# The first microseconds of a streaming-encoder kernel: halves of x in another order, the first gain row by itself, a product entered operand by operand, and three products of zeros

## What is computed

```python
z = rmsnorm(h, ln_in) @ w_in          # (640 x 1024) @ (1024 x 2464)
c_q, c_kv, k_r, g_a, u_val, u_gate, g_c = jnp.split(z, [...], axis=-1)
... # latent attention from c_q, c_kv, k_r; a depthwise convolution of u_val * sigmoid(u_gate)
h = h + jnp.concatenate([y_a, y_c], axis=-1) @ w_out
h = h + sigmoid(rmsnorm(h, ln_pg) @ w_pg) * (p @ w_pe)
```

## Time and profile before

| | us |
|---|---|
| median of three runs | 815.36 |
| the profiled execution | 814.89 |
| span of its instructions | 813.1 |
| TensorE busy | 777.2 |
| VectorE busy | 568.1 |
| ScalarE busy | 412.4 |

### The profile page before, as it was taken

The page is one execution under the profiler, slowest core; times in us unless marked ns, Lnnn a source line. Parts: engine busy times, 40 slices in busy tenths (PEclk is TensorE's granted clock), DMA queues, the critical chain, the costliest instruction groups (busy, mean ns, idle before and its releaser), DMA issues.

```text
span 813.1 us, 10487 instructions
## 1 busy us (share of the span) xinstructions
PE 777.2 (96%) x3782; PEld 603.3 (74%) x3782; DVE 568.1 (70%) x1093; ACT 412.4 (51%) x944; POOL 54.6 (7%) x94
## 2 busy tenths in 40 slices
PE   6999999999999999999999999999999999999991
PEld 4799878666766578888888988775767666888881
DVE  3349988888885685546462999889788468655455
ACT  3565645654456562363375473556445547224534
POOL 5000123000000310000000012220000000000000
PEclk9999999999999999999999999999999999999996
DMA  9622222110000153322272232121000004341203
GB/s 303 199 74 78 73 68 82 36 52 27 26 1 1 54 192 130 120 76 78 77 247 69 78 95 73 47 70 52 28 27 0 1 27 142 105 138 57 78 1 129
DMA packets 40569, 65.26 MB, mean 80 GB/s; under 512 B 7774, under 2 KB 19898, under 8 KB 40502
## 3 DMA queue, kind: packets, MB, share of 16 engines
q1 hardware_dynamic: 37354, 58.45, 22.4%
q0 software_dynamic: 3104, 6.12, 2.5%
q10 hardware_dynamic: 60, 0.02, 0.0%
HBM read 57.86 MB, written 7.17 MB: 80 GB/s over the span
## 4 chain that ended last, share of the span: by engine, by line
PE 83%; DVE 8%; ACT 6%; issue 1%; DMA 1%; SPq 0%; DVEq 0%; ACTq 0%
PE acc L600 19%; PE acc L602 19%; PE acc L601 18%; PE sharedT L534 4%; PE acc L718 4%; PE sharedO L804 4%; DVE VT L1383 3%; PE sharedS L790 3%; PE sharedT L779 3%; PE sharedS L534 2%; PE sharedO L534 2%; PE sharedT L773 1%; ACT JUNK L953 1%; PE sharedS L766 1%; ACT SB L1146 1%
## 5 line engine op out<-in xcount | busy, mean ns | idle before, releaser
L600 PE MATMUL acc<-WHI,XHI 128*128 128x512 f32 (+1 forms) x720 | 302.9, 421 | 0.6 <-DVE XLO L1328 0.6
L602 PE MATMUL acc<-WHI,XLO 128*128 128x512 f32 (+1 forms) x720 | 279.1, 388 | 0.0
L601 PE MATMUL acc<-WLO,XHI 128*128 128x512 f32 (+1 forms) x720 | 278.5, 387 | 0.0
L1383 DVE SCALAR_TENSOR_TENSOR VT<-UX,CWT,VT 128x640 f32<-128x640 f32 x240 | 211.9, 883 | 5.1
L600 PEld LDWEIGHTS acc<-WHI,XHI 128*128 128x128 f32 x720 | 135.7, 189 | 39.1 <-issue 15.2
L1318 DVE SCALAR_TENSOR_TENSOR WLO<-WR,GT,WHI 128x512 fp32r<-128x512 f32 (+1 forms) x144 | 100.1, 737 | 86.0 <-ACT WHI L957 85.7
L602 PEld LDWEIGHTS acc<-WHI,XLO 128*128 128x128 f32 x720 | 135.5, 188 | 26.7
L601 PEld LDWEIGHTS acc<-WLO,XHI 128*128 128x128 f32 x720 | 136.0, 189 | 25.7 <-issue 3.8
L957 ACT ACTIVATE WHI<-WR,GT 128x512 fp32r<-128x512 f32 (+1 forms) x144 | 94.9, 711 | 105.5 <-PE acc L602 100.6
L957 ACT ACTIVATE PT<-sharedT 128x384 f32<-128x384 f32 (+1 forms) x80 | 35.7, 447 | 43.0 <-PE sharedT L534 41.9
L1146 ACT ACTIVATE SB<-SB,NBIAS 128x384 f32<-128x384 f32 (+1 forms) x80 | 45.7, 571 | 18.6 <-DVE NBIAS L1439 18.1
(11 more groups left out here) (191 smaller groups left out, 821.2 us busy)
## 6 DMA issues: line engine op xcount, KB each, us to landing
WR<-in_w_in_dram SPq DMA_DIRECT2D x32, 256.0 KB, 3.0
WR<-in_w_in_dram SPq DMA_DIRECT2D x16, 512.0 KB, 3.5
WR<-in_w_out_dram SPq DMA_DIRECT2D x16, 512.0 KB, 3.6
WR<-in_w_pg_dram SPq DMA_DIRECT2D x16, 512.0 KB, 3.6
WR<-in_w_in_dram SPq DMA_DIRECT2D x8, 416.0 KB, 3.6
residual_spill<-H SPq DMA_DIRECT2D x5, 512.0 KB, 3.3
H<-residual_spill SPq DMA_DIRECT2D x10, 256.0 KB, 3.3
H<-in_x_prompt_dram SPq DMA_DIRECT2D x4, 512.0 KB, 7.9
```

Source lines behind the costliest of these rows:

```text
L600: mm(out, hi, w_hi, start=(first and k == 0), stop=False)
L601: mm(out, hi, w_lo, start=False, stop=False)
L602: last = mm(out, lo, w_hi, start=False, stop=(final and k == 1))
L1383: ins = stt(out=out, in0=src, scalar=w, in1=out, op0=ALU.mult, op1=ALU.add)
```

## The change

It alters only how layer 0 starts:

- `FIRST` is another list. The left halves (g = 0) of all five tiles come first, with the quanta of piece 0 between them; piece 1 follows with the right halves. The last flip, `("x", 4, 1)`, is now the last entry. SyncE loads half tiles of 256 KB in the order of `FIRST`, with the three pieces after the first, the third and the sixth of them.
- `ln_in` signals its own semaphore `gain_in`. Its eight rows are turned alone right behind the first flip (bank `gain_in`); all thirty rows are turned after the whole of `FIRST`, and VectorE copies the 22 others to `GT` after `low(2)`.
- The first quantum waits for each operand by itself (`first_hi`, `first_lo`, `w_first`) instead of for the whole split piece.
- GpSimd clears 384 columns of `TH` first; TensorE multiplies those zeros three times (128x256, into `acc[4]`, which is started afresh later) before it waits for the identity.
- The cache loads of layer 0 wait until the last half tile of x has landed.

```diff
-FIRST = [("x", 0, 0), ("x", 0, 1), ("x", 1, 0), (0, 0), ("x", 1, 1), ("x", 2, 0), (0, 1), ("x", 2, 1), (1, 0), ("x", 3, 0),
-         (0, 2), ("x", 3, 1), (1, 1), ("x", 4, 0), (0, 3), ("x", 4, 1), (1, 2), (0, 4), (1, 3), (1, 4)]
+FIRST = [("x", 0, 0), ("x", 1, 0), (0, 0), ("x", 2, 0), (0, 1), ("x", 3, 0), (0, 2), ("x", 4, 0), (0, 3), (0, 4),
+         (1, 0), ("x", 0, 1), (1, 1), ("x", 1, 1), (1, 2), ("x", 2, 1), (1, 3), ("x", 3, 1), (1, 4), ("x", 4, 1)]
+FIRST_X = [step[1:] for step in FIRST if step[0] == "x"]
...
-                eng.dma_start(ROWS[g:g + n, :], a[name][l].rearrange("(k p) -> k p", p=P)).then_inc(rows_in, 16)
+                eng.dma_start(ROWS[g:g + n, :], a[name][l].rearrange("(k p) -> k p", p=P)).then_inc(
+                    gain_in if name == "ln_in" else rows_in, 16)
...
-                for t in range(TILES):
-                    sp.dma_start(H[:, t, :], x_rows(t)).then_inc(x_in[t], 16)
-                    if t in (0, 1, 3):
-                        piece((0, 1, None, 2)[t])
+                for t, g in FIRST_X:
+                    cols = slice(512 * g, 512 * (g + 1))
+                    sp.dma_start(H[:, t, cols], x_rows(t)[:, cols]).then_inc(x_in[g][t], 16)
+                    if (t, g) in ((0, 0), (2, 0), (0, 1)):
+                        piece(((0, 0), (2, 0), (0, 1)).index((t, g)))
...
+                    begin = (i, t, k) == (0, 0, 0)
+                    if begin:
+                        pe.wait_ge(half_hi, 1)
+                        pe.wait_ge(first_hi, 1)
+                    elif (i, t, k) == (0, 0, 1):
+                        pe.wait_ge(split_ready, 1)
                     mm(out, hi, w_hi, start=(first and k == 0), stop=False)
+                    if begin:
+                        pe.wait_ge(first_lo, 1)
                     mm(out, hi, w_lo, start=False, stop=False)
+                    if begin:
+                        copied_wait(pe, (0, ("x", 0, 0)))
...
+                pe.wait_ge(warm_set, 1)
+                for _ in range(3):
+                    mm(acc[TILES - 1][:, 0:256], TH[:, 0, 0:P], TH[:, 0, P:P + 256], start=True, stop=True)
                 pe.wait_ge(ident_in, 16)
-                turn_rows(0)
...
+                turn_rows(0)
...
             if l == 0:
-                copied_wait(act, (0, "gain"))
-                high(0)
-                for t in range(TILES):
-                    for g in range(2):
-                        high_half((l, ("x", t, g)))
-                    if t == 0:
+                for t, g in FIRST_X:
+                    high_half((l, ("x", t, g)))
+                    if (t, g) == (0, 0):
+                        copied_wait(act, (0, "gain_in"))
+                        high(0)
+                    if (t, g) == (2, 0):
                         high(1)
...
             low(first_i + 2)
+            if l == 0:
+                gains(0)
...
+            nc.gpsimd.memset(TH[:, 0, 0:P + 256], 0.0).then_inc(warm_set, 1)
...
+            else:
+                pool.wait_ge(x_in[1][TILES - 1], 16)
```

More of the change, by code:

```diff
@@ L111, in cyc @@
             turn[0] += 1
[L113 to L116, removed]
+    for t, g in FIRST_X:
+        cyc((0, ("x", t, g)))
+        if (t, g) == (0, 0):
+            cyc((0, "gain_in"))
     for l in range(DEPTH):
@@ L120, in shared_bank_plan @@
                 cyc((l, ("x", t, 1)))
+        else:
+            cyc((0, "gain"))
         cyc(*((l, n) for n in ("taps", "uk0", "uk1", "st0", "st1", "p0", "p1", "p2")))
@@ L260, in build @@
         wkv_in = sem("wkv_in")
-        x_in = [sem(f"x_in{t}") for t in range(TILES)]
+        x_in = [[sem(f"x_in{half}{t}") for t in range(TILES)] for half in range(2)]
+        gain_in = sem("gain_in")
+        warm_set = sem("warm_set")
+        w_first = sem("w_first")
+        first_hi = sem("first_hi")
+        first_lo = sem("first_lo")
         filled = {b: sem(f"filled_{b}") for b in "STO"}
@@ L301, in build @@
         y_stored = sem("y_stored")
-        ROWS_IN, SQUARES, RSTDS, GATES, EXPS, H_DONE = 96, 30, 6, 35, NB + UNITS, 2 * TILES
+        ROWS_IN, SQUARES, RSTDS, GATES, EXPS, H_DONE = 80, 30, 6, 35, NB + UNITS, 2 * TILES
         CONVS, U_STORED, LATENTS_STORED = len(TAP_ORDER), 16 * (1 + NB), 64
@@ L389, in transfers @@
         def transfers(j):
-            return 2 if CHUNKS[j][1][0] == "u" else 1
+            return 2 if CHUNKS[j][1][0] == "u" and j else 1
         def raw_wait(eng, j):
@@ L407, in load_piece @@
                 for k in range(2):
-                    sp.dma_start(WR[:, j % RAW, k, :].rearrange("p (g n) -> p g n", g=2), src[:, k]).then_inc(signal, 16)
+                    sp.dma_start(WR[:, j % RAW, k, :].rearrange("p (g n) -> p g n", g=2),
+                                 src[:, k]).then_inc(signal if (j, k) != (0, 0) else w_first, 16)
                 return
@@ L541, in turn_rows @@
                 pe.wait_ge(rows_in, ROWS_IN * (to + 1))
+                pe.wait_ge(gain_in, 16 * (to + 1))
                 fill_inc(flip(bank((to, "gain"))[:, 0:30], ROWS[:, :]), (to, "gain"))
@@ L589, in quantum @@
                 first, final = c == 0, c == parts_of(name) - 1
-                if t == 0 and 0 in ks:
+                if t == 0 and 0 in ks and i:
                     pe.wait_ge(split_ready, i + 1)
@@ L626, in tensor_layer @@
                         _, t, g = step
-                        pe.wait_ge(x_in[t], 16)
+                        pe.wait_ge(x_in[g][t], 16)
                         flip_half((l, step), H[:, t, :])
+                        if (t, g) == (0, 0):
+                            pe.wait_ge(gain_in, 16)
+                            fill_inc(flip(bank((0, "gain_in"))[:, 0:8], ROWS[G_IN:G_IN + 8, :]), (0, "gain_in"))
                     else:
                         c, t = step
-                        copied_wait(pe, (l, ("x", t, 0)))
+                        if (c, t) != (0, 0):
+                            copied_wait(pe, (l, ("x", t, 0)))
                         quantum("u0", c, t)
+                turn_rows(0)
             else:
@@ L964, in high @@
                 j, raw = raw_slot(i)
-                raw_wait(act, j)
+                if i:
+                    raw_wait(act, j)
                 if i >= SPLIT:
@@ L968, in high @@
                 for k in range(2):
+                    if i == 0:
+                        act.wait_ge((w_first, w_loaded[0])[k], 16)
                     last = copy(WHI[:, i % SPLIT, k, 0:width(PARTS[i][1])], raw[:, k, :], gain_column(i, k))
+                    if (i, k) == (0, 0):
+                        last.then_inc(first_hi, 1)
                 last.then_inc(hi_ready, 1)
@@ L992, in scalar_layer @@
                 if l == 0:
-                    act.wait_ge(x_in[t], 16)
+                    for half in range(2):
+                        act.wait_ge(x_in[half][t], 16)
                 else:
@@ L1308, in gains @@
                 filled_wait(dve, (to, "gain"))
-                drain_inc(nc.vector.tensor_copy(GT[:, to, :], bank((to, "gain"))[:, 0:30]), (to, "gain"))
+                done = 0 if to else 8
+                drain_inc(nc.vector.tensor_copy(GT[:, to, done:30], bank((to, "gain"))[:, done:30]), (to, "gain"))
                 copied_wait(dve, (to, "gain"))
@@ L1314, in low @@
                 _, raw = raw_slot(i)
-                dve.wait_ge(hi_ready, i + 1)
+                if i:
+                    dve.wait_ge(hi_ready, i + 1)
                 for k in range(2):
+                    if i == 0:
+                        dve.wait_ge((first_hi, hi_ready)[k], 1)
                     at_k = (slice(None), i % SPLIT, k, slice(0, width(PARTS[i][1])))
@@ L1319, in low @@
                               in1=WHI[at_k].bitcast(F32), op0=ALU.mult, op1=ALU.subtract)
+                    if (i, k) == (0, 0):
+                        out.then_inc(first_lo, 1)
                 out.then_inc(split_ready, 1)
@@ L1331, in vector_layer @@
             if l == 0:
[L1332 to L1337, removed]
+                filled_wait(dve, (0, "gain_in"))
+                drain_inc(nc.vector.tensor_copy(GT[:, 0, 0:8], bank((0, "gain_in"))[:, 0:8]), (0, "gain_in"))
+                copied_wait(dve, (0, "gain_in"))
+                for t, g in FIRST_X:
+                    low_half((l, ("x", t, g)))
+                    if (t, g) == (0, 0):
+                        low(0)
+                    if (t, g) == (2, 0):
                         low(1)
```

## The result

The changed kernel took 820.88 us (median of 8 runs, 819.51 to 821.85), the kernel before 815.07 us (median of 8, 814.69 to 817.62). The ratio is 1.0063, 95% interval 1.0051 to 1.0074: slower, by 5.8 us between the medians and by 5.1 us by the ratio. The profiled execution took 820.29 us against 814.89, with a span of 818.5 us against 813.1: +5.4 us in both.

The account below looks back on a forecast made before the run. TensorE bounds the kernel, but ScalarE's queue sets the stretch from the last flip of x to piece 2. +3.7 (later flip) + 0.45 (slow flips) + 2.0 (half clock) = +6.1 us: 821.0 us, range 816.3 to 824.0.

Parts of the forecast that it names:

- T: Layer 0's start: last flip of x done at 28.0 us, 3.7 us later than before; extremes 25.5 and 30.5 us.
- The landing: Tile 1's left half, fourth transfer behind the identity, lands at 7.33 us, with 1088 KB in; bounds 5.64 and 9.2 us.
- The tail: From the last flip of x to piece 2, ScalarE's in-order queue takes 8.9 us, plus 0.45 for st1's half-clock flips.
- The clock: TensorE's gap before piece 2 brings the clock to 1.2 GHz when work returns, costing 2.0 us (1.4 to 3).
- The sign named beforehand: At piece 2, products 0.43 us apart for 3 us or more would show the forecast right.
- The zeros: At TensorE's start, three products of zeros take about 1.3 us, cost nothing and gain zero.
- The small parts: At the start, moved cache loads, split waits and later transfers add nothing; eight rows turn while TensorE waits anyway.
- The rule on transposes: On TensorE, transposes do not count as busy for the clock, so flips in the gap would not hold it up.
- The start's clock: First quantum at half clock takes 2.9 us; full clock up to 3 us later than before, costing 0.7 us more.
- Rival (b): ScalarE's tail does not hold piece 2, TensorE's earlier start counts fully: 810.8 to 812.2 us; chance 0.05.
- Rival (c): At the start, half-tile transfers are slow and first quanta wait for x: 823.5 us and over; chance 0.08.
- Rival (a): Clock does not fall before piece 2, or zeros give a full-clock start, or both: 817.2 us for both; chance 0.15.

Follow-up runs that it names:

- one-entry experiment: Kernel before with one entry of FIRST moved, its last flip of x placed behind the four quanta that followed it: 822.7 us, ratio 1.0089.
- caches at once: Changed kernel with the wait in front of GpSimd's cache loads taken out: 820.65 us, ratio 1.0055.
- gains first: Changed kernel with VectorE's copy of the other 22 gains ahead of low(2) instead of behind it: 819.92 us, ratio 1.0052.
- squares spread: Kernel before with tile t's mean squares behind the copies of tile t + 1, the last two behind tile 4's, high(2) after them: 814.0 us, ratio 0.9985.
- zeros throughout: Changed kernel with thirteen more products of zeros between piece 1's last product and piece 2: 818.77 us, ratio 1.0043.
- both mends and the rows together: Changed kernel with right-half flips between piece 0's quanta, mean squares behind their tiles' copies, and the first turn waiting for all six small rows: 811.39 us, ratio 0.9951.

## Why the prediction was right, step by step

Forecast 821.0, measured 820.88 us. The mechanism is the one forecast, but that the two numbers agree within 0.1 us is luck: the sum of +6.1 us stands against +5.4 us in the profiled execution, +5.8 between the medians and +5.1 by the ratio. The steps, by the profiled execution:

| | forecast | measured |
|---|---|---|
| left half of tile 1 in | 7.33 us | 7.11 us |
| last flip of x done (T) | 28.0 us | 27.84 us |
| later than before | +3.7 | +3.57 |
| T to piece 2, beyond the old 8.9 us | +0.45 | 37.14 - 27.84 - 8.88 = +0.42 |
| half clock at piece 2 | +2.0 | 6 products, 39.68 - 37.14 = 2.54 for 1.39 = +1.2 |
| sum | +6.1 | +5.2 of +5.4 |

- **The landing** was priced by bytes ahead of it. In eleven kernels of the changed kind, one profiled execution each, it came between 6.9 and 8.55 us, so 7.33 was a fair middle, with a scatter of its own that probably makes up part of the runs' scatter. The flip behind it took 1.11 us, as the earlier trace rows had it, and not the 0.88 that the forecast took; the landing, 0.22 us early, hid that, and the first product came at 8.27 us against 8.2.
- **The tail** held: the 8.9 us run from the last flip of x wherever that flip stands (24.27, 27.84 and 30.62 us in three kernels with ScalarE's order behind it untouched, the copy of `uk0` 8.1 to 8.2 us later each time). This is the step on which the sign hung, and the one-entry experiment on the kernel before shows it alone.
- **The clock** fell, in the stretch with nothing to run. Its price, 2.0 us, lies between what single executions show: 1.2 us here, where six products ran at half clock, as they did with the caches at once, and 2.2 us with the gains first, where eleven products took 41.66 - 36.97 = 4.7 us instead of 2.5 (eleven also in the kernel without zeros). The sign named beforehand, products 0.43 us apart for 3 us or more, was missed in this execution: it was 2.5 us. The changed kernel's other seven runs have mean granted clocks of 0.984 to 0.987 where the profiled one has 0.989; two of them (819.51 and 819.58 us) were faster than it all the same, so the clock alone does not order the runs.
- **The zeros** were mis-sized as work: 2.93 us for the three and not 1.3. In the trace a float32 matmul of this kind counts as two rows (three are x6), so the 16 rows from which I took 0.12 us each are 8 matmuls. It changed nothing here, since they end at 4.14 us, ahead of the first flip at 4.90 us.
- **The small parts** (caches, split waits, row by itself) were put at nothing. The experiments find nothing for the caches and the row; no run tests the split waits.
- **The range** has slips that change no step: by their own terms the extremes of T come to 5.64 + 0.88 + 10 x 1.39 + 3.5 + 0.8 = 24.7 us and 9.2 + 0.88 + 2.9 + 12.5 + 3.5 + 1.5 + 0.2 = 30.7 us, not 25.5 and 30.5, and +6.2 + 0.45 + 3.0 to 824.5 us, not 824.0.
- **The rule on transposes**, that they do not count as busy for the clock, carried no term of the sum, and the runs do not settle it. In one execution of the kernel before with its squares spread TensorE had run only the turn of the rows and three flips of x, and its first product was at full clock (the rows at 8.97 and 10.68 us above). In the kernel before and in that with its last flip last, the same four steps left the first product at half clock. So what the prediction read as agreement came from one execution and does not hold in every one.
- **The start's clock**: full at about 12.1 us, 3.9 us after the first product, which costs half, 1.9 us; the forecast had 1.4 + 0.7 = 2.1. The 0.2 us added for VectorE are there as well: the product at 15.64 us took 0.50 us in the chain, 0.26 more than its neighbours.

Rival (b) is refuted by the same rows that it named: the copy of `uk0` came 8.2 us behind T, not within 2. Rival (c) did not come up: behind the first product TensorE has no wait for x in the list. Rival (a) did not happen in the profiled execution; its first half, no fall, is what the kernel with zeros throughout makes happen. With the start at half clock that is the case for which (a) names 819 to 820 us, and it took 818.77 us.

## What to carry to other kernels

When work is moved ahead on the engine that is busy, ask which of its results another engine's in-order queue starts from, and how long that queue is from there: a flip delayed behind four quanta delayed 8 us of ScalarE's steps that had been covered until then. Such a result belongs as early as its data allows, and the queue behind it should be fed piece by piece; here the two together turned +5.1 us (1.0063) into -4.3 us (0.9947). And a gap on TensorE can have a second price beside its length: here the clock fell in it. Look for products at double spacing right behind the gap.

## What the runs showed of the hardware that I had not expected

- Products of zeros count for the clock when they run through: with thirteen of them in the gap the granted clock stayed at 1.00 for the 9 us without another product (28.35 to 37.50 us).
- Three products of zeros at the start brought the full clock once in nine profiled executions, and it was gone again before it was of use. In the kernel with both mends and the rows together the first flip took 0.63 us, the time at full clock, where it took 1.09 us in the others:

```profile
4.99 0.63 PE L547 MATMUL sharedS<-IDENT,H 128*128 128x128 f32 x4 [0.85 <-DMA H<-in_x_prompt_dram]
```

  and the windows of the same execution show half clock under the first quantum, then full clock:

```profile
7.80:11.20 3.40, 3.40 (x12) 2.46 (x10) 1.95 (x3) 1.11 (x2) 0.00 (x0) 0.51 1.07 379
11.30:14.00 2.70, 2.70 (x19) 2.36 (x18) 1.16 (x2) 2.32 (x5) 0.00 (x0) 1.00 1.07 380
```

  The Trainium skill (TensorE: Matmul & The Clock Gate, Why this matters for your kernels) advises warming up with matmuls. Here 3.8 us lay between the last product of zeros (4.14 us) and the first product (7.94 us), and the runs with and without the zeros cannot be told apart.
- The granted clock in the windows cannot be read at the start. In the changed kernel it stands at 1.00 from 7.8 to 12.0 us, where the products are 0.43 us apart. There the spacing of the products tells the clock.
- The moment at which the clock rises differs between executions of nearly the same start: it was full by the first product, at 10.7 us, in the kernel before with its squares spread, and 2.9 us behind it in the kernel before. Part of what the one profiled execution of that kernel is ahead (812.90 against 814.89 us) is such luck; the medians of 11 and 15 runs carry the verdict.
- The landing of one and the same transfer, the fourth behind the identity, moved by 1.6 us from execution to execution (6.9 to 8.55 us in eleven kernels that issue it alike).
